# Seven more landing places for the pieces of small expert units, and two pieces of the next wide unit issued early

## The reference

```python
def _moe(h, w_router, w_gate, w_up, w_down):
    logits = (x @ w_router).astype(jnp.float32)
    top_v, top_i = lax.top_k(logits, TOP_K)
    gates = jax.nn.softmax(top_v, axis=-1)
    combine = ...                       # gate of each token for each of the 8 experts
    out = jnp.zeros_like(x)
    for e in range(N_EXPERTS):
        out = out + combine[:, e:e + 1] * _swiglu(x, w_gate[e], w_up[e], w_down[e])
    return out.reshape(b, l, d)
```

## Time and profile before

| | us |
|---|---|
| median of three runs | 1407.58 |
| the profiled execution, its own time | 1405.3 |
| span of the profiled execution | 1403.5 |
| TensorE busy | 1325.2 (94%) |
| VectorE busy | 875.6 (62%) |
| ScalarE busy | 724.1 (52%) |
| weights queue (q1) of 16 DMA engines | 76.4% |
| read from HBM | 433.12 MB |

### The profile page before, as it was taken

The page is one execution under the profiler, slowest core; times in us unless marked ns, Lnnn a source line. Parts: engine busy times, 40 slices in busy tenths (PEclk is TensorE's granted clock), DMA queues, the critical chain, the costliest instruction groups (busy, mean ns, idle before and its releaser), DMA issues.

```text
span 1403.5 us, 19596 instructions
## 1 busy us (share of the span) xinstructions
PE 1325.2 (94%) x7528; PEld 1031.4 (73%) x7528; DVE 875.6 (62%) x954; ACT 724.1 (52%) x719; POOL 69.6 (5%) x92
## 2 busy tenths in 40 slices
PE   9999999999999999999997889998779998888997
PEld 8999999999999778888852258872238884226786
DVE  6554766544987699988830168860128881017897
ACT  7564544344566777777720057750027771006775
POOL 0100000000000063000000000000000000002000
PEclk9999999999999999999999999999999999999999
DMA  8563553553442799999989999989999999999992
GB/s 315 194 224 120 180 180 121 193 183 108 175 166 69 276 343 380 421 407 406 372 317 421 421 407 421 416 339 387 421 420 407 421 359 356 421 421 420 421 421 105
DMA packets 75877, 440.55 MB, mean 314 GB/s; under 512 B 7296, under 2 KB 9344, under 8 KB 30672
## 3 DMA queue, kind: packets, MB, share of 16 engines
q1 hardware_dynamic: 71680, 422.67, 76.4%
q0 software_dynamic: 3952, 16.49, 3.3%
q10 hardware_dynamic: 144, 0.02, 0.0%
HBM read 433.12 MB, written 11.01 MB: 316 GB/s over the span
## 4 chain that ended last, share of the span: by engine, by line
PE 72%; DMA 13%; DVE 7%; issue 4%; ACT 3%; SPq 0%; DVEq 0%; ACTq 0%
PE ps L2235 9%; PE ps L2236 9%; PE ps L2241 8%; DMA raw<-in_moe_w_gate 8%; PE ps L2360 7%; PE ps L1740 4%; PE ps L2259 4%; PE ps L2267 4%; PE ps L2260 4%; PE ps L1730 4%; PE ps L1731 4%; DMA raw<-in_moe_w_up 3%; PE ps L1778 2%; PE ps L1795 2%; PE ps L1779 2%
## 5 line engine op out<-in xcount | busy, mean ns | idle before, releaser
L1427 DVE TENSOR_TENSOR wl<-raw,wh 128x2048 fp32r<-128x2048 f32 x180 | 410.9, 2290 | 62.5 <-ACT wh L880 61.5
L880 ACT CAST wh<-raw 128x2048 fp32r<-128x2048 f32 x180 | 344.3, 1914 | 144.7 <-PE ps L2236 57.2
L2235 PE MATMUL ps<-wh,gh 128*128 128x512 f32 x560 | 222.0, 396 | 11.5 <-issue 8.4
L2236 PE MATMUL ps<-wh,gl 128*128 128x512 f32 x560 | 220.6, 394 | 0.0
L2360 PE MATMUL ps<-raw,few 128*64 128x512 f32 x288 | 139.3, 633 | 37.1 <-issue 28.7
L2362 PE MATMUL ps<-raw,few 128*64 128x512 f32 x312 | 155.8, 650 | 0.0
L2241 PE MATMUL ps<-wl,gh 128*128 128x512 f32 x560 | 151.3, 392 | 0.2 <-DVE wl L1427 0.2
L944 ACT ACTIVATE sil<-ps 64x512 f32<-64x512 f32 x21 | 12.4, 588 | 261.6 <-PE ps L2362 261.6
L2235 PEld LDWEIGHTS ps<-wh,gh 128*128 128x128 f32 x560 | 106.2, 190 | 37.3 <-issue 13.5
L2360 PEld LDWEIGHTS ps<-raw,few 128*64 128x64 f32 x288 | 39.2, 145 | 120.0 <-issue 120.0
L2236 PEld LDWEIGHTS ps<-wh,gl 128*128 128x128 f32 x560 | 106.2, 190 | 23.0
(11 more groups left out here) (353 smaller groups left out, 2378.2 us busy)
## 6 DMA issues: line engine op xcount, KB each, us to landing
raw<-in_moe_w_gate SPq DMA_DIRECT2D x101, 1024.0 KB, 11.3
raw<-in_moe_w_up SPq DMA_DIRECT2D x99, 1024.0 KB, 10.6
raw<-in_moe_w_down SPq DMA_DIRECT2D x88, 1024.0 KB, 12.1
raw_more<-in_moe_w_down SPq DMA_DIRECT2D x24, 1024.0 KB, 10.7
raw_more<-in_moe_w_up SPq DMA_DIRECT2D x13, 1024.0 KB, 14.1
raw<-in_diff_w_qkv SPq DMA_DIRECT2D x8, 1536.0 KB, 6.1
raw_more<-in_moe_w_gate SPq DMA_DIRECT2D x11, 1024.0 KB, 7.3
raw<-in_sb_w_qkv SPq DMA_DIRECT2D x7, 1536.0 KB, 7.7
```

Source lines behind the costliest of these rows:

```text
L880: act.copy(split_piece(wh, p), raw_piece(p)).then_inc(wh_ready, 1)
L1427: dve.tensor_tensor(split_piece(wl, p), raw_piece(p), raw_f(split_piece(wh, p)), ALU.subtract).then_inc(wl_ready, 1)
L2235: pe.matmul(ps[:, bank, :], gh[:, s], w, start=(k0 + k == 0), stop=False)
L2236: ins = pe.matmul(ps[:, bank, :], gl[:, s], w, start=False, stop=False)
```

## The change

The unused halves of `wh` and `wl` and, in a small unit, all their other halves become landing places ("spares", seven of them, tile `unsplit` over the same memory). In a small unit s7 to s13 land in spares 0 to 6; s14 and later go on in the raw slots. Spares 0 and 1 (the fourth halves) are never used for split parts, so s7 and s8 are issued with no wait; s9 to s13 wait until TensorE has used w39, w40 and w41 of the wide unit. w0 and w1 of every wide unit but the first also land in spares 0 and 1. Those of the next wide unit are issued in the midst of the small unit's list: w0 behind s37, w1 behind s39. Because w0 and w1 no longer take raw slots 0 and 1, w7 and w8 are issued with no wait. SP reads both experts' numbers at the head of its loop round. ScalarE, VectorE and TensorE do the same instructions as before with other addresses and other semaphore counts.

```diff
+SPARES, EARLY = 7, 2
...
+        def splits(own):
+            return sb("wh", [P, 2, CHUNK], F32R, where=own), sb("wl", [P, 2, CHUNK], F32R, where=own)
+        wh, wl = phase(splits)
+        unsplit = phase(lambda own: sb("unsplit", [P, 2, 2, CHUNK], where=own))
...
+        def spare(n):
+            slot = SPLIT_SLOTS if n < 2 else n // 2 - 1
+            return unsplit[:, n % 2, slot // 2, slot % 2 * PIECE:(slot % 2 + 1) * PIECE]
+        def wide_piece(a, p, first=False):
+            if p < EARLY and not first:
+                return spare(p), spare_landed[p]
+            return raw_piece(p), piece_landed[p % RAW_SLOTS]
+        def few_piece(p):
+            if RAW_SLOTS <= p < RAW_SLOTS + SPARES:
+                return spare(p - RAW_SLOTS), spare_landed[p - RAW_SLOTS]
+            return raw_piece(p), piece_landed[p % RAW_SLOTS]
...
             def load_wide(a, e, few_before):
-                for p in range(PIECES):
+                for p in range(EARLY, PIECES):
                     kind, i = unit_chunks[p // 2]
                     if few_before is not None and p < RAW_SLOTS:
                         sp.wait_ge(few_used, few_before * PIECES + PIECES + p + 1 - RAW_SLOTS)
-                    else:
+                    elif p < RAW_SLOTS or p >= RAW_SLOTS + EARLY:
                         sp.wait_ge(wl_ready, a * PIECES + C_MOE + p + 1 - RAW_SLOTS)
                     load_piece(e, p, kind, i, p % 2)
-            def load_few(v, e):
+            def load_few(v, e, after):
                 for p, (kind, i, half) in enumerate(few_pieces):
                     if p < RAW_SLOTS:
                         sp.wait_ge(wl_ready, (v + 1) * PIECES + C_MOE + p + 1 - RAW_SLOTS)
-                    else:
+                    elif p >= RAW_SLOTS + SPARES + RAW_SLOTS:
                         sp.wait_ge(few_used, v * PIECES + p + 1 - RAW_SLOTS)
-                    load_piece(e, p, kind, i, half)
+                    elif p >= RAW_SLOTS + SPARES:
+                        sp.wait_ge(few_used, v * PIECES + p + 1 - RAW_SLOTS - SPARES)
+                    elif p >= RAW_SLOTS + 2:
+                        n = p - RAW_SLOTS
+                        sp.wait_ge((wh_used, w_used)[n % 2], (v + 1) * PIECES + C_MOE + n // 2 - SPLIT_SLOTS)
+                    ...
+                    if p in after:
+                        load_early(v + 1, after[p][0], after[p][1])
+            def early(e):
+                return {PIECES - 5: (e, 0), PIECES - 3: (e, 1)}
...
             with sp.Fori(1, len(SMALL_UNITS) + 1) as v:
-                load_few(v, sp.value_load(bm["unit_i"][0:1, bass.ds(2 * v, 1)], min_val=0, max_val=E - 1))
-                load_wide(v + 1, sp.value_load(bm["unit_i"][0:1, bass.ds(2 * v + 1, 1)], min_val=0, max_val=E - 1), v)
+                few_e = sp.value_load(bm["unit_i"][0:1, bass.ds(2 * v, 1)], min_val=0, max_val=E - 1)
+                next_e = sp.value_load(bm["unit_i"][0:1, bass.ds(2 * v + 1, 1)], min_val=0, max_val=E - 1)
+                load_few(v, few_e, early(next_e))
+                load_wide(v + 1, next_e, v)
```

More of the change, by code:

```diff
@@ L293, in build @@
         piece_landed = [sem(f"piece_landed{i}") for i in range(RAW_SLOTS)]
+        spare_landed = [sem(f"spare_landed{i}") for i in range(SPARES)]
         wh_ready, wl_ready = sem("wh_ready"), sem("wl_ready")
@@ L513, in _ @@
                     e = sp.value_load(bm["unit_i"][0:1, bass.ds(a + len(SMALL_UNITS), 1)], min_val=0, max_val=E - 1)
+                    for p in range(EARLY):
+                        load_early(a, e, p)
                     load_wide(a, e, None)
@@ L872, in square_tokens, with unit_split @@
                                accum_out=small[:, 10 + n:11 + n]).then_inc(tok_squared, 1)
[L874 to L880, removed]
+            def unit_split(few, a, p, first=False):
+                piece, landed_ = wide_piece(a, p, first)
+                act.wait_ge(landed_, wide_in(a, few, p, first))
+                act.wait_ge(wh_used, split_free(a, p, first and p == 0))
+                act.wait_ge(wl_ready, split_free(a, p, first and p == 0))
+                act.copy(split_piece(wh, p), piece).then_inc(wh_ready, 1)
             for k in range(6):
@@ L900, in _ @@
                          ps[:, BACKS[n], :]).then_inc(back_ev, 1)
-            unit_split(0, 0, 1)
+            unit_split(0, 0, 1, first=True)
             def gathered_high(k):
@@ L921, in _ @@
             gathered_high(1)
-            unit_split(0, 0, 2)
+            unit_split(0, 0, 2, first=True)
             def few_gathered(v):
@@ L969, in scale_for_more, with unit_body @@
                 act.mul(part_, part_, rsT[:, n % 2:n % 2 + 1]).then_inc(tok_scaled, 1)
-            def unit_body(u, a, scatter, first=False, few_next=False):
+            def unit_body(u, few, a, scatter, first=False, few_next=False):
                 def turned_high(i):
@@ L979, in unit_body @@
                     if 2 * j + 3 < PIECES:
-                        unit_split(u, a, 2 * j + 3)
+                        unit_split(few, a, 2 * j + 3, first)
                     if kind == "d" and i + 1 < FC:
@@ L983, in unit_body @@
                     if 2 * j + 4 < PIECES:
-                        unit_split(u, a, 2 * j + 4)
+                        unit_split(few, a, 2 * j + 4, first)
                     if (kind, i) == ("g", 1):
@@ L1424, in unit_split @@
                 dve.wait_ge(wh_ready, a * PIECES + C_MOE + p + 1)
-                dve.wait_ge(w_used, split_free(a, p, first))
-                dve.tensor_tensor(split_piece(wl, p), raw_piece(p), raw_f(split_piece(wh, p)),
+                dve.wait_ge(w_used, split_free(a, p, first and p == 0))
+                dve.tensor_tensor(split_piece(wl, p), wide_piece(a, p, first)[0], raw_f(split_piece(wh, p)),
                                   ALU.subtract).then_inc(wl_ready, 1)
@@ L1493, in _ @@
             gathered_low(1, (0,))
-            unit_split(0, 1)
+            unit_split(0, 1, first=True)
             gathered_low(1, (1,))
-            unit_split(0, 2)
+            unit_split(0, 2, first=True)
             def sort_experts():
@@ L1635, in unit_body @@
                     if 2 * j + 3 < PIECES:
-                        unit_split(a, 2 * j + 3)
+                        unit_split(a, 2 * j + 3, first)
                     if kind == "u":
@@ L1648, in unit_body @@
                     if 2 * j + 4 < PIECES:
-                        unit_split(a, 2 * j + 4)
+                        unit_split(a, 2 * j + 4, first)
                     if stored and 8 <= j < 16:
```

72 lines of the change are left out of this document (48 added, 24 removed).

## The result

The changed kernel takes 1415.55 us (median of 4 runs, 1414.67 to 1417.18); the kernel before, run beside it, takes 1407.57 us (4 runs, 1405.72 to 1408.84). The ratio is 1.0059, 95% interval 1.0042 to 1.0077: slower by 8.0 us, and above the range of the prediction, which ended at 1413. The profiled execution took 1416.06 us with a span of 1414.0, 10.5 us over the span before. The medians lie 8.0 us apart; the rest of the difference is that the profiled execution of before lay 2.3 us under its median and that of after 0.5 over.

The account below looks back on a forecast made before the run. Transfers bound small units and TensorE wide ones, in a chain through s41's landing and the restart. Terms +0.2, +3.25 and -2.0 sum to +1.4 us, forecast 1409.0 us (chance 0.5), range 1401.5 to 1413.

Parts of the forecast that it names:

- The spares: Start of each small unit: s7 follows s6 without a pause, net gains 4.75, 2.35 and 2.95 us.
- Rival D: Start of small units: spares don't give s7 early because something else holds SP until T; 1418 us, chance 0.05.
- The early pieces: w0 and w1 ahead of s38 to s41: s41 lands 5.0 us later in all three small units.
- The second number at SP's head: SP's loop head: one more load of an expert's number delays small 2 and 3 by 0.6 us each.
- The restart: TensorE's start of wide 2 and 3: stays 6.4 us behind s41, the loop's jump hiding the split of w0.
- Rival B: Wide 2 and 3 start right after TensorE's last matmul, the jump having only waited for data; 1400.0 us, chance 0.18.
- Rival C: Jump's time counts from the last matmul, not s41's landing, so the half clock on s40 and s41 costs; 1411.0 us, 0.27.
- The last unit: Last wide unit: 2.42 us wait for ScalarE removed, 2.6 us of waits behind late pieces covered; its stretch net -2.0 us.
- The sign for the forecast as a whole: Wide units under 120 us would show the forecast wrong, as DMA, not TensorE, had then set them.

Follow-up runs that it names:

- e2: The kernel before with only wh and wl moved to byte 88256, their place in the changed kernel: 1415.03 us, ratio 1.0053.
- e1: The changed kernel with wh, wl and the spares placed where the kernel before has wh and wl: 1408.89 us, ratio 1.0016 against the kernel before.
- e4: e1 without the early w0 and w1, second expert number read at its old place, seven spares kept: 1401.04 us, ratio 0.9949 against the kernel before.
- e6: e4 with TensorE's and SP's loops over the small units written out: 1394.66 us, ratio 0.9911 against the kernel before.
- e7: e1 with TensorE's and SP's loops over the small units written out: 1395.63 us, ratio 0.9925 against the kernel before.
- e10: e7 with 64 unused bytes ahead of the stationary tiles, so spares, home placement and early pieces stay: 1392.56 us, ratio 0.9896 against the kernel before.

## Why the prediction was wrong, point by point

**The step that failed** stands in the description of the change and got no term at all: ScalarE, VectorE and TensorE "do the same instructions as before with other addresses", costed at nothing. The other addresses cost 3.4 ns on each of some 2460 matmuls, 8.4 us by the spacing. On the chip the placement alone made 7.8 us (e2 against before, medians) and 6.7 (the changed kernel's 1415.55 against e1's 1408.89). With the placement taken out, the kernel that I had predicted (e1) took 1408.89 us; the forecast was 1409.0. Part of that agreement is luck. Cut as the table above, the profile of e1 differs from before by +1.4 (small 1, +0.2 forecast), +3.2 (small 2, +3.25), +1.2 (wide 3, 0), +1.6 (small 3, +0.1) and -2.9 us (the last unit, -2.0). That is 4.6 us in all where 1.4 was forecast; e1's profiled execution lay 1.2 us over its median and that of before 2.3 under. The medians of the two, run beside each other, lie 1.7 us apart.

**The spares.** s7 lands 2.5 us behind s6, as predicted, in small 1, and 3.7 and 3.2 in the other two. Rival D is false. The net gain at s41 was forecast as 4.75, 2.35 and 2.95 us and measures 2.6, 1.5 and 2.3 in e4: every one is smaller. In small 1 the mis-sized term is what pushes the pieces besides the weights, which I had put at 1.35 us. From the landing of s7 to that of s41 before takes 89.0 us for 34 pieces and after 96.7 for 36; two pieces are 5.0 of the 7.7 us, and 2.7 are left. GpSimd's queue, with its store and its fetch of tokens, before (719 to 746 us) and after (724 to 746; packets, MB, share):

```profile
q0 software_dynamic: 336, 1.05, 12.0%
```

```profile
q0 software_dynamic: 336, 1.05, 14.1%
```

That is 3.2 us of the 16 engines before and 3.1 after, so the traffic is the same, and what has moved from the gap into the stream is the store. Why the stream loses twice the 1.35 us that the store's share gave is not shown. In e4 the delay stands elsewhere: s6 itself lands 3.5 us behind T in small 1, where before has 0.9.

**The early pieces.** 5.0 us at each s41 forecast, and 0.6 for the second load in small 2 and 3; 3.9, 4.8 and 5.8 measured (e1 against e4). Their whole cost, 7.9 us, and the spares' gain, 6.2, nearly cancel, which is why e1 is so near to the kernel before.

**The second number at SP's head.** 0.6 us forecast; the loads stand 0.69 us apart (930.54 and 931.23), and SP's gap from w41 to s0 is 932.06 - 924.51 = 7.55 us against 7.03, 0.5 more. Right.

**The restart.** Predicted 6.4 and 6.5 us behind s41; e1 has 6.5 and 6.4, the changed kernel 6.7 and 6.3. Rival B (the jump only waited for data) is false, by e6 and e7 as well. Rival C had half of it right: the gap of 3.07 us before s40 did bring the granted clock to its lower level, and in small 2 the last matmul ended 4.3 us behind s41 instead of 2.3. But the wide unit did not start later for it: the idle shrank to 2.04 us and the distance from s41 was 6.3. So the jump's time counts from the landing of s41, as the forecast had it. The Trainium skill gives in "Advanced Engine Details and Errata", section "ISA Cache", an instruction store of 128 KB on TensorE in lines of 16 KB (256 instructions). That a jump back costs so much because it has to fetch such a line again is a guess from it; no run here shows the fetch itself, only that the cost goes when the loop is written out.

**The last unit.** The 2.42 us of wait for ScalarE went, and of the 2.6 us behind late pieces 0.5 is left. Waits from 1280 us to the end, after:

```profile
PE ps L2376 <- DVE act L1712: 0.5, 1, 0.5
PE ps L2460 <- DMA raw_more<-in_moe_w_down: 0.5, 1, 0.5
```

For the stretch from its start to the end -2.0 was forecast and -1.0 measured, with 1.7 us of slower matmuls in it; e1, without them, has -2.9.

**A misread number.** The prediction gives 376 GB/s as part of the first dip; the slices have 372 and 317 there and no 376. No term rests on it.

**The sign for the forecast as a whole,** wide units under 120 us, did not appear in the changed kernel (122.0 us twice). e7 and e10 have it, but TensorE is busy 117.94 of 118 us there in e10, so a wide unit under 120 us does not mean that DMA sets it.

**The range** held the bounds of every cost that I had named, and none for the one that I had called free. A term of 0 for "other addresses" needed the reason that excludes a loss, and there was none in the rows.

## What to carry to other kernels

When an edit moves a tile, work out the start of every matmul operand before and after, and compare the number of matmuls in one and the same busy stretch: three matmuls fewer in 272 are 1% of TensorE's pace and were 0.6% of this kernel's time, and neither the mean duration nor any wait showed it. Test a change once with the tiles of the kernel before in their old places; its effect and the placement's are then apart. Here a wait that stood behind a loop's jump was worth nothing until the jump was gone, and the early loads that ended it delayed the pieces behind them in the queue.

## What the runs showed of the hardware that I had not expected

- **Operand starts.** For the rounded 32-bit matmuls of 128x512 with 128 stationary columns, a start 64 bytes past a multiple of 128 goes with 1.8 ns more than 227.3 if it is that of the moving or of the stationary tiles, and with 5.2 ns more if it is both. The plain float32 matmuls of the small units, which also read `unsplit`, kept their 429 ns from one to the next in all kernels. The Trainium skill, "SBUF — State Buffer", section "Operand start alignment", asks only for a multiple of the element size and says that its runs timed nothing; every start here meets that rule, and the time still differs. Which starts other than 0 and 64 cost what was not tried.
- **The loop's jump.** The branch took 5.9 to 6.2 us on TensorE, twice in every kernel with the loop. On SP the branch itself took 0.05 us, and the queue's next instruction came 5.6 us later (918.56 to 924.13). Writing out TensorE's and SP's loops together gained 6.4 us without the early pieces (e6 against e4) and 13.3 with them (e7 against e1); the two loops were not written out one by one.
- **An idle at the start of a wide unit can cost twice**: once itself, and once as matmuls spaced 426 ns instead of 229, at the lower granted clock. In wide 2 and 3 of the kernels here that start behind an idle of 2.0 to 4.6 us there are 4 to 12 of them, 0.8 to 2.4 us. It is no rule: the last wide unit of before starts behind 2.42 us and has none at its head. e10, with no idle before wide 2 and 3, has one and none, and they last 118.1 and 118.3 us.
